# Half of a merge's gate products computed beside the attention units that come before it, instead of in the merge

## What is computed

```python
# h: 512 x 1024 tokens after the pre-norm
aq, ak, av, hq, hff, hfb, hi, hg, ga, gh = split_in(h @ w_in)
o_att = window_attention(q, k, v, kc, vc, sink)     # local attention: blocks of 128, 8 heads
o_h = hgrn_bidir(...)                               # gated recurrence, both directions
def merge(o_a, o_r, g_a, g_r):
    return (sigmoid(g_a) * (o_a @ w_o_attn) + sigmoid(g_r) * (o_r @ w_o_hgrn)) @ w_out
y = merge(o_att, readout(o_h, hg), ga, gh)
```

## Time and profile before

| | |
|---|---|
| time, median of 3 runs | 4391.68 us (4389.72, 4391.68, 4398.92) |
| profiled execution | 4388.87 us, span 4387.1 us |
| mean granted TensorE clock | 0.917 of 2.4 GHz |
| busy share: PE, weight load, DVE, ACT, POOL | 90%, 75%, 38%, 32%, 26% |
| chain that ended last | TensorE for the most part; ACT, DVE, POOL and DMA the rest |
| DMA | 337 MB, 77 GB/s mean |

### The profile page before, as it was taken

The page is one execution under the profiler, slowest core; times in us unless marked ns, Lnnn a source line. Parts: engine busy times, 40 slices in busy tenths (PEclk is TensorE's granted clock), DMA queues, the critical chain, the costliest instruction groups (busy, mean ns, idle before and its releaser), DMA issues.

```text
span 4387.1 us, 52573 instructions
## 1 busy us (share of the span) xinstructions
PE 3937.4 (90%) x22131; PEld 3292.7 (75%) x22131; DVE 1646.4 (38%) x2827; ACT 1404.1 (32%) x2204; POOL 1155.8 (26%) x717
## 2 busy tenths in 40 slices
PE   6889987999998887888799989999978878998999
PEld 4778765888887776777688878888857765686888
DVE  3343554111115656556522231011247854232123
ACT  4121433312124322232342342221245534343223
POOL 2010103121123233142532342111233422243223
PEclk7787997999998998989899989999979987898999
DMA  4121123333333110111233342222232210143333
GB/s 142 58 77 31 44 69 104 106 96 102 105 93 99 39 44 25 48 39 49 77 106 105 107 116 63 63 63 63 79 103 58 63 45 10 48 122 104 98 99 106
DMA packets 471925, 336.69 MB, mean 77 GB/s; under 512 B 17529, under 2 KB 445579, under 8 KB 471691
## 3 DMA queue, kind: packets, MB, share of 16 engines
q1 hardware_dynamic: 471691, 333.34, 25.7%
HBM read 331.20 MB, written 2.10 MB: 76 GB/s over the span
## 4 chain that ended last, share of the span: by engine, by line
PE 75%; DVE 11%; ACT 4%; POOL 4%; DMA 3%; issue 3%; SPq 0%; POOLq 0%; DVEq 0%; ACTq 0%
PE PS L107 73%; DVE A L124 2%; DVE A L132 2%; PE PS L115 2%; POOL RWr L124 1%; POOL TM L124 1%; DMA RW<-in_mod_w 1%; ACT RWH L121 1%; DMA RW<-in_ffn_w_in 1%; DVE TM L132 1%; ACT A L118 1%; DVE SM L144 1%; POOL A L124 1%; DVE TM L124 1%; DVE RWr L124 1%
## 5 line engine op out<-in xcount | busy, mean ns | idle before, releaser
L124 POOL TENSOR_TENSOR RWr<-RW,RWH 128x1024 fp32r<-128x1024 f32 (+3 forms) x320 | 732.3, 2290 | 2500.5 <-ACT RWH L121 2493.7
L107 PE MATMUL PS<-HTH,RWH 128*128 128x512 f32 (+3 forms) x3376 | 1215.9, 360 | 62.8 <-POOL RWr L124 25.5
L107 PE MATMUL PS<-HTr,RWH 128*128 128x512 f32 (+3 forms) x3376 | 1191.1, 353 | 0.0
L107 PE MATMUL PS<-HTH,RWr 128*128 128x512 f32 (+3 forms) x3376 | 1189.8, 352 | 0.0
L107 PE MATMUL PS<-Ar,RWH 128*128 128x512 f32 (+1 forms) x3264 | 838.2, 348 | 32.4 <-POOL RWr L124 16.7
L107 PEld LDWEIGHTS PS<-HTH,RWH 128*128 128x128 f32 (+2 forms) x3376 | 650.0, 193 | 182.4 <-issue 72.6
L107 PEld LDWEIGHTS PS<-HTH,RWr 128*128 128x128 f32 (+2 forms) x3376 | 648.0, 192 | 87.7 <-issue 2.9
L107 PEld LDWEIGHTS PS<-HTr,RWH 128*128 128x128 f32 (+2 forms) x3376 | 650.1, 193 | 83.9 <-issue 3.1
L121 ACT ACTIVATE RWH<-RW 128x1024 fp32r<-128x1024 f32 (+2 forms) x475 | 477.0, 1007 | 671.6 <-DMA RW<-in_ffn_w_out 254.0
L107 PEld LDWEIGHTS PS<-Ar,RWH 128*128 128x128 f32 x3264 | 579.4, 196 | 124.7 <-issue 23.7
L107 PE MATMUL PS<-Ar,RWr 128*128 128x512 f32 (+1 forms) x1632 | 561.8, 344 | 0.0
(11 more groups left out here) (178 smaller groups left out, 3838.7 us busy)
## 6 DMA issues: line engine op xcount, KB each, us to landing
RW<-in_ffn_w_in SPq DMA_DIRECT2D x176, 512.0 KB, 3.9
RW<-in_mod_w SPq DMA_DIRECT2D x96, 512.0 KB, 4.2
RW<-in_w_ada SPq DMA_DIRECT2D x72, 512.0 KB, 3.7
RW<-in_ffn_w_out SPq DMA_DIRECT2D x64, 512.0 KB, 3.7
RW<-in_ffn_w_out SPq DMA_DIRECT2D x64, 384.0 KB, 3.3
RW<-in_mix_w_in SPq DMA_DIRECT2D x41, 512.0 KB, 3.9
RW<-in_ssd_w_in SPq DMA_DIRECT2D x40, 512.0 KB, 3.9
RW<-in_ev_w_in SPq DMA_DIRECT2D x24, 512.0 KB, 3.9
```

The lines of the kernel that those rows point to most:

```text
L107: return self._ins(self.real and self.real.matmul(o, l, r, start=start, stop=stop, skip_group_check=True))
L124: return self._ins(self.real and self.real.tensor_tensor(out=o, in0=i0, in1=i1, op=op))
```

## The change

The gates of the first four output features (m = 0 to 3, both x: eight products) leave the merge. Each is made in two halves of four k-tiles, step "half", and half i stands at the end of turn t = 8 + i of the attention (`steps(tail, gates)`), 16 halves in turns 8 to 23. The sigmoid of a product, step "sig", stands in the turn after its second half. The sigmoids have eight buffers instead of four: two in the working space `A` (at another place than before), two in `G0` and four in `XT`, all seen as two runs of 256 columns. The merge then begins with eight output products and goes on with m = 4 to 7 as before. Early sigmoids wait for the recurrence's last use of `G0` and `XT` ("fold"), later ones for the sum four features before instead of two. The wait for `merge.start` moves to the first copy that writes `MGH`.

```diff
-    def steps(self, tail):
+    def steps(self, tail, gates):
...
-            out += beside.get(t, [])
+            out += beside.get(t, []) + (gates[t - 8] if 8 <= t < 8 + len(gates) else [])
...
-        self.s1 = [k.A[:, 16384 + 512 * x:16896 + 512 * x] for x in range(4)]
+        halves = [x.rearrange("p (a n) -> p a n", a=2) for x in (
+            k.A[:, 16768:17280], k.A[:, 17280:17792], *(k.G0[:, 4 * i:4 * i + 4, :].rearrange("p a b -> p (a b)") for i in range(2)))]
+        self.s1 = halves + [k.XT[:, 2 * i:2 * i + 2, 512:768] for i in range(4)]
...
         for m in range(0, 8, 2):
-            out += [(self, "gate", m + f, x) for x in range(2) for f in range(2)]
+            if m > 3:
+                out += [(self, "gate", m + f, x) for x in range(2) for f in range(2)]
             out += [(self, "out", m + f, x) for f in range(2) for x in range(2)]
         return out
 
+    def early(self):
+
+        out = []
+        for i in range(8):
+            out += [[(self, "half", *divmod(i, 2), b)] + ([(self, "sig", *divmod(i - 1, 2))] if i and not b else []) for b in range(2)]
+        return out + [[(self, "sig", 3, 1)]]
+
+    def buffer(self, m, x):
+        return self.s1[2 * (m % 4) + x]
...
+        if step == "sig":
+            return
+        if step in ("gate", "half"):
             made = Product(("mg", "gate", m, x), [wp(self.w, 3328 + 1024 * x + 128 * m, 128)], (k.HTH, k.HTL), 8,
                            cover(512), ht_ready(k, self.gen))
+            if step == "half":
+                if b == 0:
+                    p.mg_made = made
+                    made.open(p, k)
+                for kk in range(4 * b, 4 * b + 4):
+                    last = p.mg_made.tile(p, k, 0, 512, kk)
+                if b:
+                    p.mg_made.close(k, last)
+                return
...
-        if step == "gate":
-            s.wait_ge_all("merge.start")
-            if m > 1:
-                s.wait_ge("v.mg", m - 2)
+        if step in ("gate", "sig"):
+            if m > 3:
+                s.wait_ge("v.mg", m - 4)
+            else:
+                s.wait_ge("pe.hg", "fold")
...
             if x:
+                s.wait_ge_all("merge.start")
                 s.wait_ge("v.mg", m)
...
-    order += hgrn.steps([("mod", 160)]) + [("mod_end", 160)] + window.steps(hgrn.finish()) + merge.steps()
+    order += hgrn.steps([("mod", 160)]) + [("mod_end", 160)] + window.steps(hgrn.finish(), merge.early()) + merge.steps()
```

More of the change, by code:

```diff
@@ L3104, in steps, with halves, tensor @@
         for m in range(0, 8, 2):
-            out += [(self, "gate", m + f, x) for x in range(2) for f in range(2)]
+            if m > 3:
+                out += [(self, "gate", m + f, x) for x in range(2) for f in range(2)]
             out += [(self, "out", m + f, x) for f in range(2) for x in range(2)]
         return out
+    def early(self):
[5 more added lines that the diff above has]
+        return self.s1[2 * (m % 4) + x]
+    def halves(self, bank):
+        return bank[:, 0:512].rearrange("p (a n) -> p a n", a=2)
     def tail(self, parts):
         return [[(self, "y", m, part) for m in range(8)] for part in parts]
-    def tensor(self, p, step, m, x):
+    def tensor(self, p, step, m, x, b=0):
         k = self.k
-        if step == "gate":
+        if step == "sig":
+            return
+        if step in ("gate", "half"):
             made = Product(("mg", "gate", m, x), [wp(self.w, 3328 + 1024 * x + 128 * m, 128)], (k.HTH, k.HTL), 8,
                            cover(512), ht_ready(k, self.gen))
+            if step == "half":
[7 more added lines that the diff above has]
+                return
         elif step == "out":
@@ L3133, in tensor, with scalar @@
         lin(p, k, made)
-    def scalar(self, s, step, m, x=0):
+    def scalar(self, s, step, m, x=0, b=0):
         k = self.k
-        if step == "gate":
-            s.wait_ge_all("merge.start")
-            if m > 1:
-                s.wait_ge("v.mg", m - 2)
+        if step in ("gate", "sig"):
[3 more added lines that the diff above has]
+                s.wait_ge("pe.hg", "fold")
             s.wait_ge("pe.lin", "mg", "gate", m, x)
-            s.act(self.s1[2 * x + m % 2], k.banks.of("mg", "gate", m, x)[:, 0:512], ACT.Sigmoid).then_inc(
+            s.act(self.buffer(m, x), self.halves(k.banks.of("mg", "gate", m, x)), ACT.Sigmoid).then_inc(
                 "s.mg_gate", m, x).frees("mg", "gate", m, x)
@@ L3145, in scalar @@
             if x:
+                s.wait_ge_all("merge.start")
                 s.wait_ge("v.mg", m)
                 s.copy(self.MGH[:, m, :], self.MG[:, m, :]).then_inc("s.mgh", m)
-        else:
+        elif step == "y":
             s.wait_ge("pe.lin", "mg", "out", 7, 1)
@@ L3153, in scalar, with vector @@
                 "mg", "y", m, x)
-    def vector(self, v, step, m, x=0):
+    def vector(self, v, step, m, x=0, b=0):
         k = self.k
         if step == "out":
-            sv = self.s1[2 * x + m % 2]
+            sv = self.buffer(m, x)
             v.wait_ge("s.mg_gate", m, x)
             v.wait_ge("pe.lin", "mg", "out", m, x)
-            v.tt(sv, sv, k.banks.of("mg", "out", m, x)[:, 0:512], ALU.mult).then_inc("v.mg_out", m, x).frees(
+            v.tt(sv, sv, self.halves(k.banks.of("mg", "out", m, x)), ALU.mult).then_inc("v.mg_out", m, x).frees(
                 "mg", "out", m, x)
@@ L3165, in vector @@
                 v.wait_ge("v.mg_out", m, 1)
-                v.tt(self.MG[:, m, :], self.s1[m % 2], self.s1[2 + m % 2], ALU.add).then_inc("v.mg", m)
+                v.tt(self.halves(self.MG[:, m, :]), self.buffer(m, 0), self.buffer(m, 1), ALU.add).then_inc("v.mg", m)
                 v.wait_ge("s.mgh", m)
@@ L3450, in plan @@
     order += post_then_head(ffn.tail(), post, pre, Head(k, [(hgrn, "q", 0), (hgrn, "v", 0)], PX), pads(8, 144))
+    order += [("mark", "hg.load"), (hgrn, "load"), ("mark", "hg.start"), (hgrn, "lb")]
     merge = Merge(k, "mix2", hgrn, window)
-    order += [("mark", "hg.load"), (hgrn, "load"), ("mark", "hg.start"), (hgrn, "lb")]
-    order += hgrn.steps([("mod", 160)]) + [("mod_end", 160)] + window.steps(hgrn.finish()) + merge.steps()
+    order += hgrn.steps([("mod", 160)]) + [("mod_end", 160)] + window.steps(hgrn.finish(), merge.early()) + merge.steps()
     post = Post(k, "p1", 1, HX, merge.Y, 1.0, lambda e, part, kk: e.wait_ge("s.yb", kk, part[0]))
```

## The result

| | before | after |
|---|---|---|
| median, us | 4396.38 (6 runs, 4389.72 to 4401.91) | 4368.87 (6 runs, 4358.40 to 4378.07) |
| ratio | | 0.9940, 95% interval 0.9922 to 0.9958 |
| span of the profiled execution | 4387.1 | 4367.6 |

The change saves 0.6%: some 26 us, and by the interval between 18 and 34 us. Runs of one kernel spread over 20 us, so the stretches of one execution tell more than its total. Busy time by stretch after the change, cut at the same instructions as in the earlier trace rows: slots 8 to 23, slots 24 to the first output product, merge up to the first product with `w_out`.

The account below looks back on a forecast made before the run. TensorE, carrying 75% of the chain that ended last, was taken to bound the kernel. Terms: -43.6 + 16.9 + 1.5 + 0.6 = -24.6 us, from 4388.9 to 4364.3; likeliest median 4366, range 4359 to 4380.

Parts of the forecast that it names:

- Clock, not idle time: In attention slots 8 to 23, only 8.6 us are idle; the gain comes from TensorE's clock rising from 0.71 to 1.00.
- units no faster: Rival: attention units keep their 62.81 us in slots 8 to 23, only idle time is won; net -8.0 us; chance 0.05.
- clock stays low: Rival: granted clock stays at 0.71 over attention slots 8 to 23; net +10.0 us (4400); chance 0.04.
- Removed: In the merge, eight of 16 gate products are taken out: 43.6 us off the path.
- the wait at the merge's start: In the merge's first output product, the third k-tile waits for DVE's last low part: 0.6 us.
- The predicted length of the merge: The merge, 131.29 us in the earlier profile, would last 88.3 us.
- Added: Attention slots 8 to 23 grow by 16.9 us, from 71.4 to 88.3 at full clock, plus 1.5 us of waiting for ACT.
- the 1.5 us for ACT: In attention slots 8 to 23, TensorE waits 1.5 us where late exponentials hold PSUM banks the next score takes.
- ACT sets the pace: Rival: ACT's 6.1 us in a 4.6 us attention slot holds TensorE up; gain only 9 to 19 us; chance 0.16.
- a value step mostly covers a late exponential: In attention slots 8 to 23, exponentials up to 1.5 us late matter for some units, mostly beside a covering value step.
- Turns 24 to 37: The attention's turns behind the filled ones, up to the merge, keep their length.
- Total: Whole kernel: 24.6 us saved, 4364.3 us for the profiled execution, new median 4366.

Follow-up runs that it names:

- adding alone: Changed kernel, but early gates are thrown away and the merge makes all sixteen; slot 3 to `w_out` 295.0 us, +18.0 on the kernel before, ratio 1.0031.
- quarters: Changed kernel with the same eight gates in pieces of six matmuls, one in each of turns 6 to 37; median 4345.84 us, ratio to before 0.9881.
- 14 loads fewer: Changed kernel with the eight early sigmoids as plain copies; slots 8 to 23 89.70 us against 89.72, ratio to the kernel before 0.9927.
- the runs with twelve gates: Changed kernel with twelve early gates in halves instead of eight; slot 3 to `w_out` 239.9 us, ratio to before 0.9917; with sigmoids as copies 236.0 us.
- fourteen gates: Changed kernel with fourteen early gates in halves instead of eight, beside slots 8 to 35; slot 3 to `w_out` 234.4 us, ratio to before 0.9900.
- eighths of four gates: Changed kernel with only four early gates, in pieces of three matmuls in turns 6 to 37; slot 3 to `w_out` 241.0 us, ratio to before 0.9914.

## Why the prediction was right

- *Clock, not idle time.* The step that carried it. The slots run at 1.00, the score matmuls at 1.37 us; adding alone costs 18.0 us for 43.6, and quarters make the filled slots shorter than the empty ones. The rivals "units no faster" and "clock stays low" are out.
- *Removed:* 43.6 less the wait at the merge's start 0.6 was 43.0; measured 42.7 to 42.8. The predicted length of the merge, 88.3 us, came out as 89.27, since the merge before was 0.8 us longer than the earlier trace rows had it. TensorE's wait for DVE in the first product after the change was 0.46 us:

```profile
3798.72 0.70 PE L107 MATMUL PS<-Ar,RWH 128*128 128x512 f32 x2 [0.46 <-DVE Ar L124]
```

- *Added:* 16.9 + 1.5 = 18.4, measured 18.3. The sum is right by luck, its parts aren't: a wait that wasn't there covers matmuls that were priced too low. TensorE waits for nothing in slots 8 to 23, so the 1.5 us for ACT was 0. Instead the matmuls need 89.7 us, not 88.3: slots with five key blocks and eight score matmuls start 4.79 us apart (3660.04, 3664.83), where 0.69 + 1.30 + 2.73 = 4.72; those with four and six start 4.47 apart, where 0.58 + 1.07 + 2.73 = 4.38. In sequence a slot costs some 0.1 us more than its pieces measured alone, and it lies in the half product (2.86 us from 3661.97 to 3664.83, where 2.73 were taken); a key block of the value steps costs 0.88 instead of 0.86.
- *ACT sets the pace:* not here; 14 loads fewer change nothing (14, not the sixteen forecast, because the eighth sigmoid stands in turn 24). That a value step mostly covers a late exponential was right. It was a real danger all the same: the runs with twelve gates show it at the first odd turn without such cover.
- *Turns 24 to 37:* unchanged as forecast. I took them as given; the runs with quarters (22.5 us) and with twelve or fourteen gates (12.5 and 18.0) show that they held much of as large a gain again.
- *Total:* 24.6 forecast, 24.6 measured from slot 3 to `w_out`; the median 4368.9 against 4366. That the medians lie so close is partly luck: the median before, 4391.7 when the forecast was made, became 4396.4 with six runs, and runs of one kernel spread over 20 us.

## What to carry to other kernels

Where TensorE runs short dependent pieces at a granted clock near 0.7, its busy time is not its work. Price the stretch at full clock, and look for independent matmuls to lay in the gaps: here the first 21.8 us were better than free, since they sped up their neighbours. Spread them over the whole slow stretch rather than part of it: quarters over 32 turns saved 22.5 us more than halves over 16, with the same matmuls. Reach did most of that, for fourteen gates in halves over 28 turns saved 18.0; and too little beside each turn is worse, for eighths of four gates, half as many matmuls over the same 32 turns, saved 11.4. And look at what is laid between two users of one PSUM bank, not only at the longest chain: the long waits that appeared in the filled slots came from there.

## What was not expected of the hardware

- Gaps of TensorE of up to 0.94 us, 3.8 of 61.8 us in all, left the clock at 1.00; with three waits of 0.5 to 2.0 us in 94.9 us it was 0.98. The Trainium skill ("TensorE: Matmul & The Clock Gate", section "A second HAM failure mode: psum-queue depth-cycling") tells of short idle times that make the clock swing; the trace agrees where nothing stands beside the units (waits of up to 1.91 us in slots 8 to 23, clock 0.71), and in the slots with eighths or quarters beside each unit it doesn't show it.
- 21.8 us of matmuls more made a stretch 2.0 us shorter (69.43 us with quarters, 71.42 before).
